# First query product of the first token tile in two halves by heads, and its expert sum closed behind the second tile's choices

## What is computed

```python
h2 = rms_norm(x, g_norm_ffn) * (1.0 + sc2) + sh2
query = (h2 @ w_query).reshape(t, 8, 2, 128)                    # 8 heads, 2 halves each
sub_scores = einsum('thpd,hpkd->thpk', query, sub_keys)         # 128 keys per half
half_vals, half_idx = top_k(sub_scores, 16)
cand = half_vals[:, :, 0, :, None] + half_vals[:, :, 1, None, :]
top_vals, top_pos = top_k(cand, 16)                             # 16 experts per head
gates = softmax(top_vals)
act = gelu(einsum('td,thkd->thk', h2, expert_down[experts])) * gates
x = x + gt2 * einsum('thk,thkd->td', act, expert_up[experts])
x = rms_norm(x, g_final)
```

## Time and profile before

| | |
|---|---|
| runs | 1640.17, 1640.22, 1643.65 us |
| median | 1640.22 us |
| profiled execution | 1638.71 us, span 1636.9 us |
| PE, DVE, ACT, POOL busy | 83%, 68%, 32%, 23% of the span |
| DMA | 433.17 MB, mean 265 GB/s |
| chain that ended last, by engine | PE 47%, DMA 25%, DVE 20%, ACT 5% |
| dot products of the experts on DVE | 256, 1224 ns each |
| gathers | 256, median 10.8 us from issue to landing |

### The profile page before, as it was taken

The page is one execution under the profiler, slowest core; times in us unless marked ns, Lnnn a source line. Parts: engine busy times, 40 slices in busy tenths (PEclk is TensorE's granted clock), DMA queues, the critical chain, the costliest instruction groups (busy, mean ns, idle before and its releaser), DMA issues.

```text
span 1636.9 us, 17137 instructions
## 1 busy us (share of the span) xinstructions
PE 1363.7 (83%) x6234; PEld 954.1 (58%) x6234; DVE 1105.7 (68%) x2021; ACT 530.1 (32%) x1024; POOL 380.5 (23%) x329
## 2 busy tenths in 40 slices
PE   6999778777767776777777778978999999899997
PEld 6887658523222222322222237867999877689996
DVE  6575574588888688888455555566765578867654
ACT  1443342222221123222111133542544254534430
POOL 1000001244444344444344411100111033001110
PEclk9999888999999999999999999999999999999999
DMA  9554525799999999999999963324465443355550
GB/s 366 203 206 154 206 78 206 275 422 405 422 421 416 417 421 406 367 422 421 421 421 421 420 265 138 120 77 168 169 206 182 173 164 109 123 180 206 182 179 26
DMA packets 116628, 433.17 MB, mean 265 GB/s; under 512 B 6832, under 2 KB 7088, under 8 KB 83520
## 3 DMA queue, kind: packets, MB, share of 16 engines
q0 software_dynamic: 36864, 268.45, 39.8%
q1 hardware_dynamic: 79392, 162.51, 28.0%
q10 hardware_dynamic: 288, 1.11, 0.2%
HBM read 431.00 MB, written 1.05 MB: 264 GB/s over the span
## 4 chain that ended last, share of the span: by engine, by line
PE 47%; DMA 25%; DVE 20%; ACT 5%; issue 2%; SPq 0%; POOL 0%; DVEq 0%; ACTq 0%; POOLq 0%
PE PS L45 45%; DMA EB<-in_experts,EI 24%; DVE EB L78 5%; DVE WL L75 4%; ACT BIG L24 2%; PE PS L84 1%; DVE LNV L63 1%; DVE Y L75 1%; DVE GV L75 1%; DMA W<-in_w_ada 1%; DVE X L63 1%; DVE XL L75 1%; ACT WH L24 1%; ACT EB L24 1%; DVE ST L69 1%
## 5 line engine op out<-in xcount | busy, mean ns | idle before, releaser
L45 PE MATMUL PS<-EB,BIG 128*128 128x512 f32 x1024 | 489.1, 622 | 168.1 <-ACT BIG L24 168.0
L45 PEld LDWEIGHTS PS<-EB,BIG 128*128 128x128 f32 x1024 | 188.8, 195 | 464.9 <-ACT BIG L24 284.5
L39 POOL DMA_INDIRECT EB<-in_experts,EI x256 | 289.6, 1131 | 602.0 <-PE PS L45 399.6
L78 DVE CUSTOM_DVE_ANT_0 EB<-EB,Y 128x1024 f32<-128x1024 f32 x256 | 313.5, 1224 | 137.4 <-DMA EB<-in_experts,EI 136.5
L75 DVE TENSOR_TENSOR WL<-W,WH 128x1024 fp32r<-128x1024 f32 x240 | 308.6, 1335 | 130.5 <-ACT WH L24 130.1
L24 ACT ACTIVATE WH<-W 128x1024 fp32r<-128x1024 f32 x240 | 237.2, 1048 | 79.5 <-PE PS L45 72.8
L45 PE MATMUL PS<-XH,WH 128*128 128x256 f32 x832 | 241.7, 291 | 11.1 <-DVE WL L75 10.5
L45 PE MATMUL PS<-XH,WL 128*128 128x256 f32 x832 | 235.5, 283 | 0.0
L45 PE MATMUL PS<-XL,WH 128*128 128x256 f32 x832 | 235.4, 283 | 0.0
L24 ACT ACTIVATE BIG<-BIG 128x2 f32<-128x2 f32 (+1 forms) x136 | 31.1, 228 | 444.9 <-DVE BIG L78 444.5
L45 PEld LDWEIGHTS PS<-XH,WH 128*128 128x128 f32 x832 | 159.8, 192 | 14.8 <-DVE WL L75 12.1
(11 more groups left out here) (170 smaller groups left out, 1405.4 us busy)
## 6 DMA issues: line engine op xcount, KB each, us to landing
W<-in_ffn_w SPq DMA_DIRECT2D x32, 2048.0 KB, 8.9
W<-in_w_ada SPq DMA_DIRECT2D x12, 2048.0 KB, 12.6
W<-in_w_in SPq DMA_DIRECT2D x6, 2048.0 KB, 12.8
W<-in_hy_w_in SPq DMA_DIRECT2D x6, 2048.0 KB, 13.7
W<-in_gla_w_in SPq DMA_DIRECT2D x6, 2048.0 KB, 7.9
W<-in_w_query SPq DMA_DIRECT2D x4, 2048.0 KB, 10.6
W<-in_w_out SPq DMA_DIRECT2D x2, 2048.0 KB, 8.0
EB<-in_experts,EI POOLq DMA_INDIRECT x256, 10.8
```

What stands on the lines that cost most here:

```text
L39: return lambda e: e.indirect_dma_start(*a, **k)
L45: return lambda e: e.matmul(*a, **k)
L78: return lambda e: e.tensor_tensor_reduce(*a, **k)
```

## The change

`score` and `first_query` work on a range of heads. For the first token tile `first_query` is called with two parts: the product with the first 256 columns (both halves of head 0), its copy, two transposes, their copy and the scores of these, and only behind the choice of head 0 in the code the same for the other 256 columns (head 1). For the second token tile it is called with one part, as before. The high and low part of wq[1]'s first piece are now issued ahead of the query's copies. In the expert loop the steps of `finish` are taken only once the choices have run out.

```diff
-        def score(t, j, tq):
+        def score(t, j, tq, i0=0, i1=4):
             b = bank()
-            for i in range(4):
+            for i in range(i0, i1):
...
-        def first_query(t, xt):
+        def first_query(t, xt, parts):
+
+            n = 4 // parts
+            ts = slice(t * 128, (t + 1) * 128)
+            for p in range(parts):
+                c, i0 = slice(p * n * 128, (p + 1) * n * 128), p * n
+                b = bank()
+                tk = dense(PS[b][:, c], wq[0], lambda k: parts3((XH[:, k, ts], XL[:, k, ts]), (wq[0].hi[:, k, c], wq[0].lo[:, k, c])),
+                           *xt, *bank_free[b])
...
+                ta = act(lambda e: e.activation(STG[:, c], PS[b][:, c], ACT.Copy), tk, t_wout, *(stg_free if t else ()), ordered=False)
...
+                yield
...
+                for i in range(i0, i0 + n):
+                    tk = tr(PS[b][:, i * 128:(i + 1) * 128], STG[:, i * 128:(i + 1) * 128], ta, *bank_free[b])
...
+                yield
+                yield score(t, 0, tq, i0, i0 + n)
...
         norm_x1.give(1, groups[1, 1], 1, t_wout, turn=False)
-        query = first_query(0, (norm_x1.xt[0],))
+        query = first_query(0, (norm_x1.xt[0],), 2)
+        later_split(wq[1])
+        tick(1)
         next(query)
-        later_split(wq[1])
         later_split(wq[2])
         next(query)
-        tick(1)
         norm_x1.last()
         t_xt = norm_x1.tokens
         next(query)
         for step in choose(0, 0, 1):
             step()
+        for _ in query:
+            pass
         drain()
...
-        query = first_query(1, t_xt)
+        query = first_query(1, t_xt, 1)
...
-                next(fin, None)
+                if chosen:
+                    next(fin, None)
```

More of the change, by code:

```diff
@@ L1145, in score @@
             ts = act(lambda e: e.activation(
-                BIG[:, 4096 + t * 2048 + j * 512:4096 + t * 2048 + (j + 1) * 512], PS[b][:, :], ACT.Copy), tk, ordered=False)
+                BIG[:, 4096 + t * 2048 + j * 512 + i0 * 128:4096 + t * 2048 + j * 512 + i1 * 128],
+                PS[b][:, i0 * 128:i1 * 128], ACT.Copy), tk, ordered=False)
             bank_free[b] = (ts,)
@@ L1151, in build @@
         stg_free = []
-        def first_query(t, xt):
[L1155 to L1170, removed]
+        def first_query(t, xt, parts):
[6 more added lines that the diff above has]
+                           *xt, *bank_free[b])
+                if t:
+                    wdone(wq[0], tk)
+                ta = act(lambda e: e.activation(STG[:, c], PS[b][:, c], ACT.Copy), tk, t_wout, *(stg_free if t else ()), ordered=False)
+                bank_free[b] = (ta,)
+                yield
+                b = bank()
+                for i in range(i0, i0 + n):
+                    tk = tr(PS[b][:, i * 128:(i + 1) * 128], STG[:, i * 128:(i + 1) * 128], ta, *bank_free[b])
+                stg_free[:] = [tk]
+                tq = act(lambda e: e.activation(QT[0][:, i0:i0 + n, ts], PS[b][:, c].rearrange("p (c t) -> p c t", c=n), ACT.Copy),
+                         tk, t_wout, ordered=False)
+                bank_free[b] = (tq,)
+                yield
+                yield score(t, 0, tq, i0, i0 + n)
         def top16(src, vals, idx, *tokens):
```

## The result

| | median, us | lowest to highest | runs | profiled execution | its span |
|---|---|---|---|---|---|
| before | 1639.21 | 1637.11 to 1643.65 | 14 | 1638.71 | 1636.9 |
| changed | 1632.71 | 1630.07 to 1636.75 | 14 | 1636.0 | 1634.2 |

The ratio is 0.9961, with a 95% interval of 0.9951 to 0.9970: the change takes 6.4 us off, between 4.9 and 8.0. I had predicted 1631.1 and a gain of 9.1. The time lies 1.6 us above the prediction and in the range, but the gain is smaller than the sum of my two terms, and the interval leaves that sum out. The prediction stood on a median of three runs, 1640.22 us; the fourteen runs of before give 1639.21.

What follows compares the result with a forecast made beforehand. The expert phase was taken as bound by gather bytes, leaving its start and holes to win: 4.2 + 4.9 = 9.1 us off the 1640.22 us median gives 1631.1 us, range 1627.8 to 1636.2.

Steps and rivals of the forecast that it cites:

- the likeliest case: Whole kernel: both gains arrive as worked out, 1628 to 1633.5 us, predicted at 1631.1 us; chance 0.68.
- Part 1: Start, up to gather 6: first query product in two halves, predicted gain 4.2 us, ends 1.5 and 5.5.
- part 2: Expert stream: first tile's closing moved behind the choices, predicted gain 4.9 us, ends 0 and 5.3.
- First choice: DVE's choice for the first head, before gather 6: to start at 240.7 instead of 244.72, 4.0 us earlier.
- PE's wait ... gone or under 1.5 us: Sign of being right: PE's wait ahead of the first group of wq[1] gone or under 1.5 us.
- up to 1.6 us: PE's group after the first choice: 18 products at 0.12 us instead of 0.21 could return this much more.
- PE takes DVE's place: Rival at the start: PE at low clock reaches its group at 256, first gain 0 to 2; chance 0.12.
- The hole: Gathers 133 to 157: 65.1 us where 59.8 are needed, so the old closing among the choices costs 5.3 us.
- Lateness: Gathers 186 to 196, beside the moved closing: at most 3 us late, against a ring slack of 2.9 us.
- the slower rival: After the moved closing TensorE's clock stays low; slower from 14 such gathers on, 1647 us with 18; chance 0.03.
- a stretch under 380 GB/s near 785 to 805: Sign of the moved closing's gain being wrong: DMA rate below 380 GB/s at about 785 to 805 us.
- no cheaper behind the choices: Rival in the expert stream: the moved closing gains only 0 to 2 us, time 1635.0 us; chance 0.10.

Runs made afterwards that it cites:

- changed_again: The changed kernel run a second time with no edit; median 1633.11 us, ratio to before 0.9964.
- halves_only: The changed kernel with the first tile's closing (steps of `finish`) put back among the choices; ratio to before 0.9975.
- halves_without_piece_first: The changed kernel with the first piece of wq[1] split at its old place, product halves and moved closing kept; ratio to before 0.9958.
- closing_only: The kernel before with only the closing (steps of `finish`) moved behind the choices; ratio to before 0.9996.
- before_constants_after: The kernel before with only the load of the second block's constants and lambda moved behind the last gather; 1635.96 us, ratio 0.9983.
- constants_after_stream: The changed kernel with the second block's constants and lambda loaded once the last gather has landed; 1629.62 us, ratio to before 0.9943.
- closing_after_stream: The changed kernel with the first tile's closing taken out of the expert loop and put behind the last gather; ratio to before 1.0033.

## Why the prediction was right, and where it was not

The time came out in the range and in the likeliest case, and that is in part luck. Part 1 gave about 1 us more than predicted and part 2 about 3 less, and the base of 1640.22 us was itself 1.0 us above the median of fourteen runs. From 1639.21 the same sum gives 1630.1, 2.6 us below what was measured. Point by point:

- **First choice.** Predicted 4.0 us earlier; 12.77 to 8.72 us behind the start of the product is 4.05. All steps under it (piece at 236.0, low part at 239.4, lows at 240.7) ended within 0.5 us of their numbers. Right.
- **Part 1, 4.2 us.** It measured 5.1 to 5.2 at gather 6 in eight traces and 4.2 in the first. The step that was off was PE: I put it at the next group at 250.4 to 254.4, in the middle 253, so that some of DVE's 4 us would be lost. The second half ran at full clock (0.12 us apart), and so did the second tile's product, and PE was there at 250, ahead of DVE. My sign of being right, "PE's wait ... gone or under 1.5 us", is thereby missed, 2.13 us, and harmlessly so: it is the early end of my own bounds. What comes on top of the choice's 4.05 us is the clock, the "up to 1.6 us" of which I had taken only a little: the group takes 4.00 us from its start to the transposes behind it before (256.75 to 260.75), 3.09 in changed_again at the full clock and 3.87 in the first profile, so 0.9 and 0.1 us. The time agrees: halves_only took 4.1 us off, interval 2.5 to 5.7.
- **PE takes DVE's place** (a rival) did not come: PE was early. Next to the choice stand ACT's seven high parts, which end with it to a tenth of a microsecond; I had not looked at them. They don't bind, as each low part needs only its own high part.
- **Part 2, 4.9 us.** This is the term that failed. From gather 6 to the last (the table's last column less "front") the stream takes 645.20 us before; the move takes 1.1 to 2.3 us off it in four traces (changed, changed_again, halves_without_piece_first, closing_only; 1.9 in changed_again, 1.7 in closing_only). The missing 3 us have three places. The hole gave 4.5 us and not 5.3: gathers 133 to 157 now hold one late landing of 0.95 us, of the kind told of in the last section. Gathers 157 to 181 hold another, 0.9 us. Both stand at the same two dot products (140 and 162) in all ten traces without the hole and in none of the four with it (the 61.11 of halves_only is a landing elsewhere); my sum had nothing for them. The rest is in gathers 181 to 201. The moved closing cost 0 to 1.1 us beside the constants, where I said 0.4, in 0 to 1.0. And I had the load at nothing: "its 1.1 MB are 2.6 us of bytes that are paid either way, and they keep the DMA fed". With lambda they are 1.25 MB and 3.0 us, which is what the load cost before; in a stream without the hole the stretch loses 4.5, with no closing in the loop. But the load is not the main cause: with it moved behind the stream in both kernels, the stream takes 642.41 us with the old closing and 640.06 with the moved one (before_constants_after, constants_after_stream), so that the move is worth 2.35 us even there.
- **Lateness.** Predicted at most 3 us for gathers 186 to 196. Against the pace of gather 181, number 193 is issued 8.4 us late (796.24 us, 38.22 for twelve gathers of 2.487), 3.0 of it the constants' bytes. I had counted DVE's and PE's waits with PE at full clock. But the rows of before had shown the clock at 0.50 in this very stretch, and I used that only for the slower rival. Ahead of transposes an up at the low clock stands in the way: 3.46 us for two. The prediction's own sign of part 2 being wrong, "a stretch under 380 GB/s near 785 to 805", came with it: 283 and 274 GB/s.
- **The rival "no cheaper behind the choices"** had the place and the kind right (constants, transposes that hold back ups) and a gain of 0 to 2 for part 2; with 1.1 to 2.3 the truth is at its upper end. I gave it 0.10, too little. By the whole time it would have been 1635.0; a larger part 1 made up for it.
- **Slower by a low clock that stays** did not come: from 810 to 960 us the clock is 0.99, as before.
- **The Trainium skill's rule** (DMA: Bandwidth & Descriptors, anatomy of one DMA on the GpSimd path) would have had the old closing nearly free, and moving it worth nothing. The hole of 4.5 us is real in every trace that has the closing among the choices, and gone in every one that has not. That closing_only gained 0.7 us in time, which can't be told from nothing, is no support for the rule: the gain was made and spent again.

What is not settled: why the second pause follows the constants only where the hole is gone. The kernels with the hole had 52.71 to 52.73 us there, three times; those without it, no closing near, 54.19 and 54.35. That a late landing is at this place is seen. The traces offer a candidate: an 8 KB packet of instructions, which the last section tells of, comes at dot product 182 in the kernels with the hole, just ahead of the load's own pause, and at 185 to 188 in those without. Whether it costs nothing in the one place and a pause in the other was not tested.

## What to carry to other kernels

In a stream that is bound by its bytes, a hole removed can come back in part further on (here 4.5 us became 1 to 2), so add up the whole stream, from its first to its last transfer, and not the hole. Load what is wanted only later into the first stretch in which the transfer engines are idle: inside the stream its bytes cost their full time (3.0 us for 1.25 MB), and behind them TensorE paused for 3.2 us and came back at the low clock. The load's new place gave 2.8 and 3.4 us in two kernels, more than moving the closing did. Where the view of the chain passes an engine that ended a tenth of a microsecond behind another, ask the code which of the two the next step waits for. And when the expected gain is near what two executions differ by, measure distances from an event that both traces have, and take the profile of the changed kernel twice.

## What the runs showed of the hardware

Gathers in a full stream do not come evenly. They land 2.487 us apart, and at a few points the whole stream steps back by 0.95 us for good. DVE's dot products show it, as they start when a gather has landed; two dot products of closing_after_stream that follow on each other, 3.45 us apart where all others around are 2.49:

```profile
785.87 1.23 DVE L78 CUSTOM_DVE_ANT_0 EB<-EB,Y 128x1024 f32<-128x1024 f32 x1 [1.26 <-DMA EB<-in_experts,EI]
...
789.32 1.23 DVE L78 CUSTOM_DVE_ANT_0 EB<-EB,Y 128x1024 f32<-128x1024 f32 x1 [1.78 <-DMA EB<-in_experts,EI]
```

In the DMA view of 786 to 789 us of that kernel there is one packet of another queue (queue, kind: packets, MB, share):

```profile
q0 software_dynamic: 175, 1.26, 100.9%
q14 instruction: 1, 0.01, 0.6%
```

Its steps, in dots near 609, 665, 721, 789 and 895 us, all have such an instruction packet of 8 KB within 5 us ahead of them. The steps belong to places in the program and not to times. Dot product 118 (counted from 0, as the gathers) is late in all fourteen traces, and 140 and 162 are in the ten without the hole, each 2.4 us behind such a packet, although gather 6 is issued anywhere from 302.47 to 310.13 us. With the closing out of the loop, and its instructions with it, the step at 226 is at 230, and its packet has moved along. It is not the rule that each packet makes a step: those near 640, 708 and 764 us made none, nor did one at 722 to 726 us in the kernel before, and from 783 to 800 us, where before loses nothing beyond the constants, it has none. Nor does each step have an 8 KB packet: halves_only loses 1.5 us at dot product 166 with only a packet of 16 KB ahead. So the steps go with instruction transfers; that they are made by them was not tested.

The Trainium skill, Runtime: NRT & Kernel Launch, section on instruction fetch mechanics, has the fetch of instructions running ahead by itself and hidden by the rate at which an engine starts instructions. That does not speak of a queue of transfers that is full; in this stream 0.95 us appear beside the packet.

The clock of TensorE is not the same twice. Behind the same wait of 2.1 us the same program ran a group of 18 products at 0.12 us from start to start in one execution (full clock, with two waits of 0.16 us), and in another at 0.21 (the low one) from the seventh on, which is 0.9 of the 1.0 us between the two front stretches of the changed kernel.
